# Compression stage of a hybrid decoder kernel: page requests tied to the unit ahead, and the copies shared out anew

## What is computed

```python
def compress_blocks(rows, pe, w1, w2):
    B, L = rows.shape[:2]
    nb = L // CMP_BLK
    blk = rows[:, :nb * CMP_BLK].reshape(B, nb, CMP_BLK, 2, NSA_KV_HEADS, NSA_HEAD_DIM)
    h = jax.nn.silu(jnp.einsum('bnlcgd,lcde->bncge', blk + pe[:, :, None, :], w1))
    return jnp.einsum('bncge,cef->bncgf', h, w2)

# nsa_sample:
cmp_past = cache_cmp_kv[li, page_table].reshape(B, past_len, 2, G, D)
ckv = jnp.concatenate([compress_blocks(cmp_past, pe, w1, w2),
                       compress_blocks(cmp_kv, pe, w1, w2)], axis=1)
```

## Time and profile before

| | us |
|---|---|
| median of 3 runs | 1750.44 (1748.89 to 1755.62) |
| the profiled execution, its time | 1752.28 |
| its span in the trace | 1750.5 |
| the stage of the change in the trace | 173.7 to 305.8 |

### The profile page before, as it was taken

One profiled execution on the slowest core, in us unless ns is written; L12 is line 12 of the kernel. 1 busy time (PEld: TensorE's weight loads), 2 busy tenths in 40 slices (PEclk: granted clock), 3 DMA queues, 4 the chain that ended last, 5 costly groups with the idle time before them and its releaser, 6 DMA issues. The chain is left out here.

```text
span 1750.5 us, 35364 instructions
## 1 busy us (share of the span) xinstructions
PE 1588.2 (91%) x13664; PEld 1401.5 (80%) x13664; DVE 759.5 (43%) x1418; ACT 640.0 (37%) x1186; POOL 740.7 (42%) x522
## 2 busy tenths in 40 slices
PE   6998476698899888999999999998998999999997
PEld 6998466466576577999999988987667899999997
DVE  2211335555455559232233268127559623223235
ACT  3222456355454425422222224226533532222322
POOL 6641442433255446643444426503136644334330
PEclk8999788799999889999999999998989999999999
DMA  8336886364455643433333213324215233323311
GB/s 241 112 85 163 268 274 190 100 184 150 121 179 154 184 121 121 161 117 121 108 120 97 81 52 87 100 72 145 85 44 150 85 110 95 92 85 101 90 32 49
DMA packets 295263, 215.47 MB, mean 123 GB/s; under 512 B 33924, under 2 KB 287416, under 8 KB 294328
## 3 DMA queue, kind: packets, MB, share of 16 engines
q1 hardware_dynamic: 279464, 180.70, 34.4%
q0 software_dynamic: 8496, 22.68, 4.1%
q10 hardware_dynamic: 7136, 9.83, 2.2%
HBM read 200.95 MB, written 20.55 MB: 127 GB/s over the span
## 5 line engine op out<-in xcount | busy, mean ns | idle before, releaser
L1731 POOL TENSOR_TENSOR w_own_t<-w_raw,w_own_t 128x1024 fp32r<-128x1024 f32 (+1 forms) x106 | 251.2, 2377 | 252.3 <-ACT w_own_t L1859 252.3
L1566 PE MATMUL ps<-x_parts,w_own_t 128*128 128x512 f32 x608 | 221.0, 402 | 9.2 <-POOL w_own_t L1731 8.7
L1840 PE MATMUL ps<-x_parts,w_own_t 128*128 128x264 f32 x608 | 173.2, 285 | 0.0
L1842 PE MATMUL ps<-x_parts,w_own_t 128*128 128x264 f32 x608 | 172.6, 284 | 0.0
L1841 PE MATMUL ps<-x_parts,w_own_t 128*128 128x264 f32 x608 | 172.6, 284 | 0.0
L1568 PE MATMUL ps<-x_parts,w_own_t 128*128 128x256 f32 x608 | 172.3, 283 | 0.0
L1859 ACT CAST w_own_t<-w_raw 128x1024 fp32r<-128x1024 f32 (+1 forms) x106 | 107.6, 1025 | 116.0 <-PE ps L1842 100.6
L1731 POOL TENSOR_TENSOR w_low_ahead<-w_raw,w_high_ahead 128x1024 fp32r<-128x1024 f32 (+1 forms) x40 | 95.1, 2381 | 129.5 <-ACT w_high_ahead L1859 129.5
L1566 PEld LDWEIGHTS ps<-x_parts,w_own_t 128*128 128x128 f32 x608 | 116.4, 191 | 35.9 <-POOL w_own_t L1731 9.5
L755 PE MATMUL ps<-flat,w 64*64 64x128 f32 (+1 forms) x2048 | 76.2, 313 | 53.3 <-ACT flat L539 50.4
L755 PEld LDWEIGHTS ps<-flat,w 64*64 64x64 f32 x2048 | 72.3, 158 | 57.6 <-issue 50.0
(11 more groups left out here) (424 smaller groups left out, 4371.0 us busy)
## 6 DMA issues: line engine op xcount, KB each, us to landing
w_raw<-in_ffn_w_gu SPq DMA_DIRECT2D x88, 512.0 KB, 3.7
pages<-in_cache_slc SPq DMA_DIRECT2D x192, 128.0 KB
rows<-in_cache_cmp SPq DMA_DIRECT2D x130, 128.0 KB, 5.8
w_raw<-in_ffn_w_down SPq DMA_DIRECT2D x32, 448.0 KB, 3.7
w_raw<-in_gla_w_in SPq DMA_DIRECT2D x24, 512.0 KB, 3.6
rows<-in_cache_cmp POOLq DMA_DIRECT2D x84, 128.0 KB, 6.0
pages<-in_cache_slc POOLq DMA_DIRECT2D x64, 128.0 KB, 2.9
w_raw<-in_ffn_w_down SPq DMA_DIRECT2D x16, 512.0 KB, 4.0
```

What stands on the lines that cost most here:

```text
L1566: nc.tensor.matmul(bank[:, 0:2 * FOLD].rearrange("p (a n) -> p a n", a=2), high, parts[2][:, :, at, 0:FOLD], start=(k == 0), stop=False)
L1731: nc.gpsimd.tensor_tensor(low(u)[:, 0:k], raw[:, u % RAW, 0:k], high(u)[:, 0:k].bitcast(F32), ALU.subtract).then_inc(low_done, 1)
L1840: nc.tensor.matmul(psum(i), high(u)[:, k, :], a[0][:, at, c], start=(k == 0), stop=False)
L1842: ins = nc.tensor.matmul(psum(i), low(u)[:, k, :], a[0][:, at, c], start=False, stop=(k == t.kc - 1))
```

## The change

- `ROW_SHARE`: SyncE 14 pages, ScalarE 13, GpSimd 5.
- `pe_cmp` is requested ahead of `w1`.
- VectorE copies the chunks 0, 1, 3, 4, 5 and 7, GpSimd 2 and 6, ScalarE none. GpSimd's copies of unit n stand ahead of its requests for unit n+2; at unit 0 its two copies stand ahead of its requests for unit 1, too.
- `load_part` waits for one thing more: that of the unit ahead (n-1) all pages but the last two of each of the three shares have landed (`most_rows`).
- ScalarE's order is now: sigmoid of unit n-1, requests for unit n+2, sigmoid of unit n. Its requests for unit 1 begin with the stage.

```diff
-ROW_SHARE = (0, 14, 20, ROW_UNIT)
+ROW_SHARE = (0, 14, 27, ROW_UNIT)
...
-                    act.dma_start(w1[64 * hf:64 * hf + 64, c], io["nsa_w_cmp1"][0, :, c]).then_inc(cst["w1_in"][c], 16)
+                    act.dma_start(S["pe_cmp"][64 * hf:64 * hf + 64, c], io["nsa_pe_cmp"][0, :, c, :]).then_inc(cst["rows0_in"], 16)
             for c in range(2):
                 for hf in range(2):
-                    act.dma_start(S["pe_cmp"][64 * hf:64 * hf + 64, c], io["nsa_pe_cmp"][0, :, c, :]).then_inc(cst["rows0_in"], 16)
+                    act.dma_start(w1[64 * hf:64 * hf + 64, c], io["nsa_w_cmp1"][0, :, c]).then_inc(cst["w1_in"][c], 16)
...
-    CD, RING = 4, 4
+    CD, RING, LEFT = 4, 4, 2
     CH = D // 2 // CD
+    BY_POOL = (2, 6)
+    BY_DVE = tuple(j for j in range(CH) if j not in BY_POOL)
...
-        def load_part(eng, n, by, arrived):
+        def load_part(eng, n, by):
 
             if n >= 2:
-                eng.wait_ge(flat_act, CH // 2 * (n - 1))
-                eng.wait_ge(flat_dve, CH // 2 * (n - 1))
+                eng.wait_ge(flat_pool, len(BY_POOL) * (n - 1))
+                eng.wait_ge(flat_dve, len(BY_DVE) * (n - 1))
+                for part, there in enumerate(most_rows):
+                    eng.wait_ge(there[(n - 1) % 2], 16 * (SHARE[part + 1] - SHARE[part] - LEFT) * (n // 2))
             for m, page in zip(range(SHARE[by], SHARE[by + 1]), S["next_pages"][by]):
                 c = UN[n][0]
+                arrived = (most_rows if m < SHARE[by + 1] - LEFT else rest_of_rows)[by]
...
         def _(pool):
-            for n in range(1, len(UN)):
-                load_part(pool, n, 2, rows_sw)
+            for n in range(len(UN)):
+                for j in BY_POOL:
+                    flatten(pool, nc.gpsimd.tensor_copy, n, j, flat_pool)
+                if n == 0:
+                    load_part(pool, 1, 2)
+                if n + 2 < len(UN):
+                    load_part(pool, n + 2, 2)
...
             for n in range(len(UN)):
-                for j in range(0, CH, 2):
-                    flatten(act, nc.scalar.copy, n, j, flat_act)
-                    if j == 2 and n:
-                        sigmoid(n - 1)
+                if n:
+                    sigmoid(n - 1)
...
-                for j in range(1, CH, 2):
+                for j in BY_DVE:
                     flatten(dve, nc.vector.tensor_copy, n, j, flat_dve)
                     if j == 1 and n:
                         activate(n - 1)
```

More of the change, by code:

```diff
@@ L485, in phase_compress @@
                            for i, n in enumerate(("other", "pre", "sig")))
-        rows_sp, rows_act, rows_sw = ([sem("rows_%s%d" % (n, s)) for s in range(2)] for n in ("sp", "act", "sw"))
+        most_rows, rest_of_rows = ([[sem("%s_rows_%s%d" % (some, n, s)) for s in range(2)] for n in ("sp", "act", "sw")]
+                                   for some in ("most", "rest_of"))
         w2_in, pm_in = sem("w2_in"), sem("pm_in")
-        flat_act, flat_dve, chunk_done, other_done, pre_done, sig_done, hid_done = (
-            sem(n) for n in ("flat_act", "flat_dve", "chunk_done", "other_done", "pre_done", "sig_done", "hid_done"))
+        flat_pool, flat_dve, chunk_done, other_done, pre_done, sig_done, hid_done = (
+            sem(n) for n in ("flat_pool", "flat_dve", "chunk_done", "other_done", "pre_done", "sig_done", "hid_done"))
         bias_done, ck_done, ckx_done = sem("bias_done"), sem("ck_done"), sem("ckx_done")
@@ L520, in rows_there @@
                 return
-            for by, arrived in enumerate((rows_sp, rows_act, rows_sw)):
-                eng.wait_ge(arrived[n % 2], 16 * (SHARE[by + 1] - SHARE[by]) * (n // 2 + n % 2))
+            for by in range(3):
+                eng.wait_ge(most_rows[by][n % 2], 16 * (SHARE[by + 1] - SHARE[by] - LEFT) * (n // 2 + n % 2))
+                eng.wait_ge(rest_of_rows[by][n % 2], 16 * LEFT * (n // 2 + n % 2))
         def flatten(eng, copy, n, j, done):
@@ L527, in flatten @@
             dst = flat[k % RING]
-            if j < 2:
+            if j in (BY_POOL[0], BY_DVE[0]):
                 rows_there(eng, n)
@@ L543, in _ @@
             for n in range(1, len(UN)):
-                load_part(sp, n, 0, rows_sp)
+                load_part(sp, n, 0)
             for name in ("mask_s", "gsum", "expand", "tri"):
@@ L574, in _ @@
                 if n == 0:
-                    load_part(act, 1, 1, rows_act)
+                    load_part(act, 1, 1)
                     for c in range(2):
@@ L580, in _ @@
                 if n + 2 < len(UN):
-                    load_part(act, n + 2, 1, rows_act)
+                    load_part(act, n + 2, 1)
                 if n == 4:
                     act.wait_ge(cst["cmp_out"], 16 * 4)
-                    act.wait_ge(flat_dve, CH // 2 * len(EX))
+                    act.wait_ge(flat_dve, len(BY_DVE) * len(EX))
+                    act.wait_ge(flat_pool, len(BY_POOL) * len(EX))
                     for g in range(G):
@@ L749, in _ @@
                         beside[n, j]()
-                    pe.wait_ge(flat_dve if j % 2 else flat_act, k // 2 + 1)
+                    if j in BY_POOL:
+                        pe.wait_ge(flat_pool, len(BY_POOL) * n + BY_POOL.index(j) + 1)
+                    else:
+                        pe.wait_ge(flat_dve, len(BY_DVE) * n + BY_DVE.index(j) + 1)
                     for e in range(CD):
```

## The result

| | before | after |
|---|---|---|
| median | 1750.87 us (8 runs, 1742.01 to 1755.62) | 1760.61 us (8 runs, 1758.94 to 1765.23) |
| profiled execution, its span | 1752.28, 1750.5 | 1760.50, 1758.8 |
| stage in the trace | 173.7 to 305.8 | 176.5 to 316.3 |
| all behind the stage | 1444.7 | 1442.5 |
| last landing of unit 7 | 292.4 | 301.6 |

The time went up: ratio 1.0065, 95% interval [1.0047, 1.0082], +9.7 us by the medians and +8.2 by the two profiled executions. The stage ends 10.5 us later. What follows it is 2.2 us shorter in this execution; among the fourteen profiled executions that part lies between 1439.6 (a_pool_2_4) and 1446.6 (a_split_dve_all), so it is not put down to the change.

A forecast was written before the change was run, and what follows sets the result against it. The prediction took ScalarE's own queue of requests, page reads and copies to bound the stage. Start 0, unit 7's landing +6.3 and tail +0.7 gave +7.0 us, median 1757.4, forecast 1758; own range 1751 to 1766, overall 1740 to 1772.

The forecast's parts named there:

- rivals for faster and for no change: Stage: transfer sets the pace, 1737, chance 0.15; or lateness and early start cancel, 1752, chance 0.1.
- Part 1: Stage start: `pe_cmp` first finishes unit 0 about 8 us earlier, all spent in ScalarE's queue: 0.
- Part 2: Units 2 to 7: sigmoids behind ScalarE's requests and reads, requests behind the unit ahead; unit 7 lands 6.3 us later.
- the landing of its last pages less 2.6 us: Even units: next unit's requests start 2.6 us before the last landing, six pages left at 0.44 us each.
- Part 3: GpSimd's chunk copies: 2.4 us each, hidden in even units, tail after unit 7's landing 14 against 13.3: +0.7 us.
- GpSimd's copy is the new bound: Rival, GpSimd's chunk copies: at 4.6 us each, +13 on top of +7, 1770; chance 0.2.
- Exclusion of VectorE and GpSimd: Copies of both engines counted one after the other; tail 10.6 us without, 15.4 with full exclusion, 14 taken.
- paced by the transfer: Rival, stage's page loads: unit 1 lands at 194, each next 14.1 us later, unit 7 at 278.6; 1737, chance 0.15.

The follow-up runs named there:

- a_pool_2_4: After, with GpSimd copying chunks 2 and 4 of a unit in place of 2 and 6; 1760.20 us, ratio 1.0061 to before.
- a_split_dve_all: a_split with VectorE copying all eight chunks of a unit and GpSimd none; 1752.60 us, ratio 1.0012 to before.
- b_pe_first: The kernel before, with `pe_cmp` requested ahead of `w1` and nothing else changed; 1751.98 us, ratio 1.0002 to before.
- a_spread_first_reads: After, with ScalarE's thirteen page reads for unit 1 moved in two portions into earlier idle time of the projection; 1761.28 us, ratio 1.0068 to before.
- a_dve_all_no_follow: a_split without the wait for the unit ahead and with VectorE copying all eight chunks; 1744.62 us, ratio 0.9974 to before.
- a_split: After, with ScalarE's requests cut into six, the sigmoid, then seven and the reads, score copies ahead of unit 6's requests; 1752.31 us, ratio 1.0019 to before.
- a_late_reads: After, with ScalarE's page reads for units 4 and 6 moved behind the next sigmoid; 1755.83 us, ratio 1.0039 to before.

## Why the prediction came out as it did

The forecast was 1758, slower, with 1751 to 1766 as its own range; the time is 1760.6. Its rivals for faster and for no change did not occur. Step by step:

- **Part 1, the start is worth nothing.** Right, and b_pe_first shows it for that edit alone. But the reason given, 8 us spent in ScalarE's queue, was wrong. TensorE started at 178.17, 1.7 us behind the stage's start (some 2 forecast). ScalarE's requests for unit 2 waited for unit 1's pages until 196.3, not for its own queue, and the sigmoid of unit 0 came at 204.1 (206.5 forecast) and hardly held VectorE. The requests for unit 3 came at 212.36, as forecast (212.1) by accident: GpSimd's request there was released by the landing of unit 2, so the transfer and the new wait set the time. Not foreseen was the stage's later start by 2.8 us, from seven more page reads at the end of the projection; a_spread_first_reads showed that it costs nothing.
- **Part 2, requests and reads ahead of the sigmoid.** Right in mechanism and prices. 13 requests took 8.64 us (8.5), 13 reads 7.3 (7.3), the sigmoid came 16.0 us after the first request (15.8), VectorE waited 10.8 and 11.0 us in the even units (10), and the DMA was idle ahead of units 4 and 6. Requests for unit 4 at 232.5 (231.9), unit 4 landed at 249.5 (248.6).
- **The term that was mis-sized** is "the landing of its last pages less 2.6 us", the lead of the next requests by the new wait. With two pages of each share open, six in all, I took 6 x 0.44. Requests for unit 5 came at 248.6, 0.9 us ahead of the landing at 249.5. GpSimd's five pages had all landed by 244.3, so four pages were open at most; and of the 192 landing signals that the wait counts from SyncE's pages (16 each) 188 had come by 246.9, the last only at 248.4, so a few stragglers took what was left of the lead. That made unit 4's turn 1.7 us longer and the sigmoid 264.1 in place of 261.8. Unit 6 landed at 284.5 (282.8). The requests for unit 7 came at 284.8 (282.1), released by VectorE's last copy of unit 5, which took 2.08 us beside GpSimd's and ended at 284.56; unit 7 landed at 301.6 (298.8): +9.1 in place of +6.3.
- **Part 3, GpSimd's copy.** 1.95 us alone, below the 2.4 taken; 2.41 in the mean with the hold-ups, so the term fitted for another reason. The Trainium skill (GPSIMD Engine Reference, section 7) gave 2.5, an estimate, by its cost for reads that step over 8 bytes; the trace's 1.95 decides against it for this copy. The tail is 14.7 us (14 taken, 13.3 before). Rival "GpSimd's copy is the new bound" fell: TensorE waited 10.5 us in all for it, and a_pool_2_4, which shortened the worst copy by half, moved nothing.
- **Exclusion of VectorE and GpSimd.** Counted one after the other, and the rows show that: 4.75 us beside three copies, 5.72 at 205.33 us, and 3.30 for one of VectorE's behind GpSimd's requests and copy. One of the forecast's grounds was misread. The mean of 973 ns for VectorE's eight adds is no steady slowing: seven took 0.70 us with GpSimd working beside them, and one took 2.89. In the kernel before, VectorE's timeline and then GpSimd's have:

```profile
37.70 2.89 DVE L415 TENSOR_TENSOR qrT<-by_sin,by_cos 128x520 f32<-128x520 f32 x1
```

```profile
37.63 2.40 POOL L248 TENSOR_TENSOR pw_low<-w_raw,pw_high 128x1024 fp32r<-128x1024 f32 x1 [2.01 <-ACT pw_high L352]
...
44.25 2.95 POOL L248 TENSOR_TENSOR pw_low<-w_raw,pw_high 128x1024 fp32r<-128x1024 f32 x1 [2.49 <-ACT pw_high L352]
```

GpSimd began 0.07 us ahead of the long add, which ended 0.56 us behind it; at 44.25 it began 0.01 us behind the next add, and its own operation took 0.55 us longer. So the one that came second waited, which supports the exclusion better than the mean did. The Trainium skill (SBUF — State Buffer, "Who interferes with whom") has it that, with VectorE in a two-port mode, one of the two blocks the other for the whole instruction; the runs add that GpSimd got no turn between VectorE's copies that follow each other. What it costs in time hides in after; in the kernel with timely sigmoids and no wait it may be 4.2 us, by intervals that overlap.
- **Rival "paced by the transfer".** Its rate, 14.1 us a unit, was nearly reached by a_dve_all_no_follow (14.4 and 14.7), with three things undone: the sigmoid's place, the wait, GpSimd's copies. Its claim that timely sigmoids alone would do it is refuted by a_split, 16 us a unit. And what it said of unit 1 (194) fails too: 197 to 200 in all kernels with `pe_cmp` ahead and the new order, so 287.3 is the last landing and not 278.6.

The sum, +7.0, was +8.2 in the profiled executions: +9.1 for unit 7's landing and +1.4 for the tail, less 2.2 us behind the stage that no step explains.

## What to carry to other kernels

A request and an index read cost an engine time in its own order (0.65 and 0.56 us here), so look for what stands behind a run of them: a sigmoid of 0.4 us stood 16 us behind the start of 13 of each, and the order of six requests, the sigmoid, seven requests, with the score copies moved too, got 8 of the 10 us back. Taking work off an engine that is busy 37% does nothing if what is left on it comes late. A wait that orders transfers can look free while something else is later: here its removal gave nothing in after and 6.6 us once sigmoids and copies were out of the way. So test such edits together.

## What was not expected of the hardware

- GpSimd's strided copy of 128x1024 takes 1.95 us alone, as long as ScalarE's (1.97) and less than its own two-input operation of that size (2.44).
- A GpSimd copy that meets a row of VectorE's copies gets no turn between them. The longest (GpSimd's timeline of after) has VectorE's copies of unit 1 beside it until 209.29:

```profile
205.33 5.72 POOL L546 COPY flat<-rows 128x1024 f32<-128x1024 f32 x1
```

- A transfer that is asked for earlier can arrive later: unit 1 landed at 204.9 in b_pe_first, 195.6 in the kernel before. Unit 2's pages were asked for while it was still under way; with the wait in their way it landed at 198.4, so 6.5 of the 9.3 us go with them.

Three things stay open: how a_split's gain over a_late_reads divides between the requests and the score copies, which that kernel moved together; whether the wait and GpSimd's copies cost more together than one by one; and why the part behind the stage varies by 7 us between executions.
